# A hymba layer with a 16-expert MoE: router on unnormalized rows, shorter rank products, the first two experts preloaded

## What is computed

```python
h = h + mixed @ w_out
t = rms_norm(h, norm_ffn_g)
group_prob = softmax(t @ w_group + b_group)                 # 4 groups
gp, gi = top_k(group_prob, 1)
exp_logits = (t @ w_expert + b_expert).reshape(-1, 4, 4)    # 16 experts
ev, ei = top_k(exp_logits[chosen group gi], 2)
ew = softmax(ev) * gp
y = zeros_like(t)
for e in range(16):
    y = y + gates[:, e:e+1] * ((silu(t @ w_gate[e]) * (t @ w_up[e])) @ w_down[e])
h = rms_norm(h + y, final_norm_g)
```

## Time and profile before

| | |
|---|---|
| Time, median of 3 runs | 1294.54 us (1292.42 to 1296.68) |
| The profiled execution | 1298.6 us, with a span of 1296.7 us inside it |
| Mean granted TensorE clock | 0.931 of 2.4 GHz |
| PE busy (multiplying) | 1118.7 us, 86% of the span, 6954 instructions |
| DVE busy | 811.0 us, 63% |
| ACT busy | 619.7 us, 48% |
| POOL busy | 351.9 us, 27% |
| Moved by DMA | 208.54 MB, mean 161 GB/s |

### The profile page before, as it was taken

How to read it: one execution, slowest core, us unless ns; L and a number is a source line. 1 busy time by engine, 2 the same in 40 slices (tenths; PEclk the granted TensorE clock), 3 DMA queues, 4 the chain that set the end, 5 groups by cost and what they waited for, 6 DMA issues and landing times.

```text
span 1296.7 us, 21172 instructions
## 1 busy us (share of the span) xinstructions
PE 1118.7 (86%) x6954; PEld 887.6 (68%) x6954; DVE 811.0 (63%) x1201; ACT 619.7 (48%) x976; POOL 351.9 (27%) x230
## 2 busy tenths in 40 slices
PE   4899999999969689999999448999999999999920
PEld 4899899999957355555555337777777777777710
DVE  4697656444395454543433446788778888888828
ACT  5422111276423354433332116777667777777712
POOL 1431211122101001111112013544444445444332
PEclk9799999999979799998999659999999999999965
DMA  6365222222154500111113728785997958664056
GB/s 243 143 236 85 65 74 75 83 65 84 23 112 182 182 1 1 50 49 49 49 50 114 298 82 317 244 297 213 370 372 276 367 195 316 233 224 164 16 173 264
DMA packets 90051, 208.54 MB, mean 161 GB/s; under 512 B 8288, under 2 KB 28256, under 8 KB 89328
## 3 DMA queue, kind: packets, MB, share of 16 engines
q1 hardware_dynamic: 78464, 165.69, 37.7%
q0 software_dynamic: 8064, 29.36, 6.4%
q10 hardware_dynamic: 3456, 12.58, 2.4%
HBM read 222.71 MB, written 40.94 MB: 203 GB/s over the span
## 4 chain that ended last, share of the span: by engine, by line
PE 60%; DVE 11%; ACT 10%; issue 7%; POOL 5%; DMA 3%; SPq 2%; ACTq 1%; POOLq 0%; DVEq 0%
PE ps L462 17%; PE ps L2078 15%; PE ps L1746 9%; ACT split L2121 5%; POOL split L2040 5%; PE ps L1719 3%; PE ps L1696 3%; DVE split L2174 2%; DVE mem L2258 1%; PE ps L1713 1%; PE ps L1733 1%; PE ps L1357 1%; PE ps L537 1%; PE ps L2066 1%; ACT mem L1639 1%
## 5 line engine op out<-in xcount | busy, mean ns | idle before, releaser
L2078 PE MATMUL ps<-split 128*128 128x512 f32 x1728 | 428.0, 402 | 28.9 <-DVE split L2174 21.1
L2078 PEld LDWEIGHTS ps<-split 128*128 128x128 f32 x1728 | 321.5, 191 | 117.8 <-DVE split L2174 20.0
L2121 ACT CAST split<-weights 128x1024 fp32r x288 | 293.8, 1050 | 125.9 <-PE ps L2078 84.9
L2174 DVE TENSOR_TENSOR split<-weights,split 128x1024 fp32r<-128x1024 f32 x216 | 281.7, 1357 | 92.4 <-ACT split L2121 92.2
L462 PE MATMUL ps<-xsplit,wsplit 128*128 128x384 f32 (+2 forms) x1584 | 280.5, 333 | 6.7 <-DVE xsplit L416 6.7
L462 PEld LDWEIGHTS ps<-xsplit,wsplit 128*128 128x128 f32 x1584 | 256.9, 194 | 13.2 <-DVE xsplit L416 7.6
L2040 POOL TENSOR_TENSOR split<-weights,split 128x1024 fp32r<-128x1024 f32 x72 | 188.1, 2612 | 239.9 <-ACT split L2121 239.9
L246 POOL TENSOR_TENSOR wsplit<-mem,wsplit 128x1024 fp32r<-128x1024 f32 x22 | 57.8, 2629 | 251.3 <-ACT wsplit L315 251.3
L1746 PE MATMUL ps<-mem 128*128 128x512 f32 x256 | 119.4, 611 | 0.8 <-DVE mem L1585 0.8
L1557 DVE TENSOR_REDUCE sml<-ps 128x1 f32<-128x1040 f32 (+7 forms) x64 | 46.6, 769 | 84.9 <-PE ps L1696 84.8
L1639 ACT COPY mem<-ps 128x512 f32<-128x512 f32 (+3 forms) x48 | 21.5, 481 | 136.0 <-PE ps L1713 90.2
(11 more groups left out here) (382 smaller groups left out, 1290.2 us busy)
## 6 DMA issues: line engine op xcount, KB each, us to landing
weights<-in_w_down SPq DMA_DIRECT2D x25, 2048.0 KB, 7.8
weights<-in_w_gate SPq DMA_DIRECT2D x48, 1024.0 KB
weights<-in_w_up SPq DMA_DIRECT2D x48, 1024.0 KB
ye_d<-par ACTq DMA_DIRECT2D x24, 512.0 KB, 7.4
mem<-in_w_in SPq DMA_DIRECT2D x22, 512.0 KB, 4.1
ye_d<-mem POOLq DMA_DIRECT2D x16, 512.0 KB, 11.2
mem<-in_x SPq DMA_DIRECT2D x10, 512.0 KB, 4.3
mem<-in_w_out SPq DMA_DIRECT2D x1, 4096.0 KB, 12.9
```

The costliest lines, as they stand in the source:

```text
L2078: mm = nc.tensor.matmul(ps[:, bank + h, :], x, w[place % RING][:, 512 * h:512 * h + 512], start=(k == 0 and p_ == 0), stop=(k == n - 1 and ...
L2121: nc.scalar.copy(WH[place % RING], raw(kind, k, q)).then_inc(wh_ready, 1)
L2174: nc.vector.tensor_tensor(WL[place % RING], raw(kind, k, q), WH[place % RING].bitcast(F32), ALU.subtract).then_inc(wl_dve, 1)
```

## The change

1. The router no longer waits for the norm. PE transposes the residual rows `H1R` themselves; the norm's gain is multiplied into the router's matrix `WRT` once (POOL), and the 1/rms of each row into the logits (DVE). The last tile's "x" and "r" entries move two steps up. `XN2` is still written and stored for the experts, and SP reloads an `H1R` buffer only after its transposes were copied (`ring_free`).
2. Ranks: the counts over all tiles are summed by PE (8 products of 16 columns, bf16), and the ranks over tiles as well (8 more, of 128 down to 16 columns), in place of DVE's seven additions and copies. The one-hot tables for the row numbers are bf16, and the row number is split in two parts below 256, so that one pass is exact; the 16 products start after the first half of the table `HOTR`.
3. Experts 0 and 1 always get at least one block. Expert 1's weights are loaded into buffer 1 before the routing's tables exist, and the load tables count both as present. The first block's addresses are fixed in the program.
4. The first block's chunks are split during the routing: ACT makes the high parts of chunks 0 to 3 behind its two exponentials, DVE the low part of chunk 0 while PE counts and of chunks 1 and 2 behind the row numbers, POOL that of chunk 3. ACT no longer waits for `tables_ready` before the first block.

The core of the diff:

```diff
@@ attention
-        NSTEP = NJOB + 11
+        NSTEP = NJOB + 9
-            return ... 4 * n + {"m": 7, "x": 13, "r": 14}[kind]
+            return ... 4 * n + {"m": 7, "x": 13 - 2 * (n == NT - 1), "r": 14 - 2 * (n == NT - 1)}[kind]
 def sp_attention
                     sp.wait_ge(h1_stored[p % 2], 16 * (p // 2 + 1))
+                    sp.wait_ge(ring_free, xt_at[p])
                     sp_residual(sp, p + 2)
 def pool_attention
+            pool.wait_ge(ffn_loaded, 48)
+            nc.gpsimd.tensor_tensor(WRT, WRT, par[:, P_GMIX:P_GMIX + KD].unsqueeze(2).to_broadcast([P, KD, 20]), ALU.mult).then_inc(pool_filled, 1)
 def dve_normed
-                dve.wait_ge(ring_free, xt_at[p - 2])
 def act_square
+            if p >= 2:
+                act.wait_ge(xn2_stored[p % 2], 16 * (p // 2))
-            nc.scalar.activation(XT2[:, p % 2].rearrange("p k q -> p (k q)"), H1R[:, p % 2], ACT.Square,
+            nc.scalar.activation(XN2[:, p % 2], H1R[:, p % 2], ACT.Square,
 def pe_ring, "x"
-                pe.wait_ge(xn2_ready, n + 1)
+                pe.wait_ge(h1_ready, n + 1)
-                    mm = nc.tensor.transpose(b[:, P * j:P * j + P], XN2[:, n % 2, P * k:P * k + P], ident)
+                    mm = nc.tensor.transpose(b[:, P * j:P * j + P], H1R[:, n % 2, P * k:P * k + P], ident)
@@ def pe_route
-            nc.tensor.matmul(ps[:, 0, 0:P], con[:, C_TRI:C_TRI + P], f, start=True, stop=True)
-            nc.tensor.matmul(ps[:, 0, P:2 * P], con[:, C_ONES:C_ONES + P], f, start=True, stop=True).then_inc(rank_done, 1)
+            for t in range(NT):
+                mm = nc.tensor.matmul(ps[:, 3, 0:NE], ALL, OKB[:, t], start=(t == 0), stop=(t == NT - 1))
+            mm.then_inc(rank_done, 1)
+            nc.tensor.matmul(ps[:, 0, 0:P], BEFORE, OKB.rearrange("p t e -> p (t e)"), start=True, stop=False, skip_group_check=True)
+            for t in range(NT - 1):
+                mm = nc.tensor.matmul(ps[:, 0, NE * (t + 1):P].rearrange("p (t e) -> p t e", e=NE), ALL,
+                                      OKB[:, t].unsqueeze(1).to_broadcast([P, NT - 1 - t, NE]), start=False, stop=(t == NT - 2),
+                                      skip_group_check=True)
+            mm.then_inc(rank_done, 1)
             for n in range(2 * NT):
-                mm = nc.tensor.matmul(ps[:, 1, 0:NB], HOTR[:, n], HOTB[:, n], start=(n == 0), stop=(n == 2 * NT - 1))
+                if n == NT:
+                    pe.wait_ge(slot_hot_ready, 2)
+                mm = nc.tensor.matmul(ps[:, 1, 0:2 * NB], HOTR[:, n], HOTB[:, n].rearrange("p i b -> p (i b)"), start=(n == 0), stop=(n == 2 * NT - 1))
@@ def dve_route
-            link(tt(LG, LGR, BR.unsqueeze(1).to_broadcast([P, NT, 20]), ALU.add))
+            link(tt(LG, LGR, RS2.unsqueeze(2).to_broadcast([P, NT, 20]), ALU.mult))
+            link(tt(LG, LG, BR.unsqueeze(1).to_broadcast([P, NT, 20]), ALU.add))
+            dve_weights_lower(dve, None, 0, "gu", 0, 0)
             dve.wait_ge(rank_done, 1)
...
+            link(ts(BLK[:, 0:2], BLK[:, 0:2], 1.0, None, ALU.max))
...
-            for t in range(1, NT):
-                link(tt(PRE[:, t], PRE[:, t - 1], TOT[:, t - 1], ALU.add))
...
+            for k in range(2):
+                tt(HOTR[:, NT * k:NT * k + NT], fl[0][:, NT * k:NT * k + NT].to_broadcast([P, NT, P]),
+                   IOTAP.unsqueeze(1).to_broadcast([P, NT, P]), ALU.is_equal).then_inc(slot_hot_ready, 1)
...
+            dve.wait_ge(idx_done, 1)
+            link(ts(IXF, ps[:, 1, NB:2 * NB], float(P), None, ALU.mult))
+            tt(ixb, ps[:, 1, 0:NB], IXF, ALU.add).then_inc(slots_ready, 1)
+            for k in range(1, RING - 1):
+                dve_weights_lower(dve, None, k, "gu", k, 0)
...
-            link(ts(NEW[:, 0:1], EBF[:, 0:1], 0.0, None, ALU.is_gt))
+            link(stt(NEW, EBF, 1.5, NEW, ALU.is_gt, ALU.mult))
@@ def sp_experts
+            sp.wait_ge(out_done, NT)
+            for half in range(2):
+                for i, w in enumerate(("w_gate", "w_up")):
+                    sp.dma_start(WGU[:, KD + 4 * half:KD + 4 * half + 4, i],
+                                 a[w][1, 512 * half:512 * half + 512].rearrange("(k p) n -> p k n", p=P)).then_inc(w_loads[half], 16)
...
-            sp.wait_ge(ring_free, len(ring))
+            sp.wait_ge(ring_free, xt_at[NT - 1])
+            sp.wait_ge(first_loaded, 32)
             sp.dma_start(WDN[:, 0:FF // P], a["w_down"][0]...).then_inc(first_loaded, 16)
+            sp.wait_ge(rt_gap, 1)
+            sp.dma_start(WDN[:, FF // P:2 * FF // P], a["w_down"][1]...).then_inc(wdn_loaded, 16)
             sp.dma_start(H1, h1_d.rearrange("(t p) d -> p t d", p=P)).then_inc(late_loaded, 16)
@@ def act_experts
+            act.wait_ge(out_done, NT)
+            act.wait_ge(first_loaded, 32)
+            for k in range(RING):
+                higher(None, k, "gu", k, 0)
+            act.wait_ge(slots_ready, 1)
             copy_x(0, 0)
+            for k in range(RING, KD):
+                higher(None, k, "gu", k, 0)
+            silu(0, 0)
             act.wait_ge(tables_ready, 1)
-            act.wait_ge(first_loaded, 48)
```

More of the change, by code:

```diff
@@ L1945, in raw @@
         def raw(kind, k, q):
+            if isinstance(q, int):
+                return WGU[:, q * KD + k].rearrange("p i n -> p (i n)")
             if kind == "gu":
@@ L2001, in body @@
                 for half in range(2):
-                    if par or not first:
-                        sp.wait_ge(w_loads[half], 32 * b)
+                    sp.wait_ge(w_loads[half], 32 * b + 32)
                     sp.wait_ge(chunk_used, (free, free_second)[half])
@@ L2008, in body @@
                                      cond=new).then_inc(w_loads[half], 16)
-                if par or not first:
-                    sp.wait_ge(wdn_loaded, 16 * b)
+                sp.wait_ge(wdn_loaded, 16 * b + 16)
                 sp.wait_ge(chunk_used, free_down)
@@ L2194, in dve_experts @@
             x_lower(0, 0)
-            q0 = buffer_of(dve, 0)
-            for k in range(KD):
+            for k in range(RING, KD):
                 if k % RING < RING - 1:
-                    lower(None, k, "gu", k, q0)
+                    lower(None, k, "gu", k, 0)
             hidden(0, 0)
```

83 lines of the change are left out of this document (40 added, 43 removed).

## The result

The changed kernel takes 1280.1 us (median of 4 runs, 1276.69 to 1284.37), the kernel before, run beside it, 1295.6 us (4 runs, 1292.42 to 1298.81): the ratio is 0.9882, 95% interval 0.9838 to 0.9926. So the change gains 15 to 18 us. Single executions scatter by more than the 0.3% named at the start: the kernel before alone ran from 1282.9 to 1303.2 us beside the kernels of this document, but for one execution in a slower state (1487.97 us at a mean granted clock of 0.725), which is left out everywhere.

The account below looks back on a forecast made before the run. PE bounds the experts, so the end follows the first expert product: router 3.9 less 0.36, ranks 4.8, entry 6.6 make 14.9 us. 1298.6 becomes 1283.7; less 4.1 for the median, 1279.6 (range 1273.5 to 1286.5).

Parts of the forecast that it names:

- Router: Last tile's router on PE: not waiting for the norm gains 3.9 us, the added multiplication on the logits costs 0.36.
- Counting products: PE's 8 bf16 products of 16 columns for the ranks: 0.16 us each, 1.3 together.
- Lock: In the ranks, POOL's split of chunk 3 holds up DVE's first product of two SBUF tables: 1.8 us lost.
- The tables for the row numbers: DVE's HOT, its scaling, two halves and HOTR in two halves, ahead of the row products: 4.5 us.
- Row numbers: End of the ranks, when the row numbers are there: 747.1 us instead of 755.44, 8.3 earlier.
- Landing: First gather of rows for the experts, beside bulk loads: lands after 5.5 us, 1.0 to 1.2 more than before.
- Rival (b): The gather is late, queued among 12 MB of new bulk loads, landing 4.0 over the one assumed: 1283.4 us, chance 0.13.
- The first two experts without tables: Part of the stretch from the row numbers to the first expert product, for which 6.6 us gained was claimed.
- Rival (a): Passage lighter than reckoned: no lock cost, clock up through the router, quick small products; 4.2 less, 1275.4 us, chance 0.16.
- Rival (c): In the experts, the third expert's weights come late, costing 5 to 6 us: 1285.1 us, chance 0.05.
- (d): In the experts, weight loads set the pace after all and the gain is given back: 1294.5 us, chance 0.02.
- (e): In attention, six residual reloads behind the transposes' copies eat up the gain and 3.9 more: 1298.4 us, chance 0.02.

Follow-up runs that it names:

- after_again: The changed kernel once more, unchanged, timed against the kernel before: 1277.3 us, ratio 0.9866.
- undo_router: The changed kernel with only the router's part undone (it waits for the normalized rows again, no multiplication by 1/rms): 1283.2 us, ratio 0.9894.
- before_again: The kernel before once more, unchanged, profiled a second time: 1296.5 us (1 run).
- pool_late: The changed kernel with only POOL's split of chunk 3 moved from the routing to behind the tables: 1274.8 us, ratio 0.9840.
- splits_wait: splits_late, with ACT waiting for the tables and the first block's skipped loads before it splits, as in the kernel before: 1279.6 us, ratio 0.9905.
- best: both_late, with DVE taking the low part of the first block's rows in the middle of the tables: 1274.0 us, ratio 0.9870.
- both_late: The changed kernel with POOL's first-block splits behind gathers and tables, and the residual's 4 MB load issued behind the tables: 1274.3 us, ratio 0.9872.
- splits_late: The changed kernel with no first-block chunk split during the routing, all split after the rows are copied: 1278.7 us, ratio 0.9870.

## Why the prediction was right, and where its terms were not

The time (1280.1 and 1277.3 for 1279.6) and the passage (40.27 for 758.75 - 718.62 = 40.13) came out, with a rest 2.5 us shorter in the profiled execution. Four terms were mis-sized, three by 0.7 to 0.9 us too long and one by 2.5 too short, and cancelled: that the passage came out within 0.1 us of its sum (0.8 in after_again) is luck.

- **Router** (3.9 gained, 0.36 paid): right, 3.4 net by undo_router. Leaving the 16 products at 3.57 was the cautious bound: 2.86 and 1.93 were measured, so 0.7 and 1.6 more were gained. The sum took the fall from a row of the kernel before, at 721, 2.8 us behind the residual; in before_again the same program had it at 4.1, and in the change it came while the products ran.
- **Counting products** (8 of 0.16, 1.3 us): 0.41, and the second half of the row products (1.4) 0.61. The Trainium skill's rule (TensorE: Matmul & The Clock Gate, Back-to-back issue gap), which I had only weighed, was nearer. By it, an estimate, 0.2 us were due; measured were 0.41, 0.05 per product of 16 columns. DVE's split of chunk 0, "hides in PE's work" in my sum, then became what ends the wait: PE is done at 736.23, the split at 736.76. The nearest row, an f32 product of 32 columns, was a poor guide for bf16 products of 16. (The sum's 734.95 should also read 734.86, 732.76 + 0.80 + 1.3.)
- **Lock** (1.8 lost): 1.7, as a whole: its mechanism and its size. It hit the second product rather than the first, since DVE was there 1.6 us sooner and POOL only 0.7. The product ended 0.14 us behind POOL's split (741.12 and 740.98), and without that split, in pool_late, it took 0.29. That agrees with the Trainium skill's exclusive lock (SBUF — State Buffer, Who interferes with whom) and not with even sharing.
- **The tables for the row numbers** (4.5): 742.32 to 746.83, 4.5. The scaling with one tensor operand took 0.49 for the 0.72 taken (L1872); the rest of the sum made up for it.
- **Row numbers** (747.1, rel. 28.5): rel. 26.86, sooner by 1.6, by the terms above.
- **Landing** (5.5, "1.0 to 1.2 more"): 8.0, so 3.5 more than before. This is the step that failed. I had the bulk loads end at 755, when the gather would be nearly in; the last of them, issued at 735.81, landed 30.1 us later, at 765.9 (the queues moved some 410 GB/s until 764), so the gather stood beside them over its whole way. (Of the 12 MB that the rival called new, 6 were there before too, but had landed before that gather.) I priced it by the median of the gathers in the expert stage, where the traffic is 253 GB/s on average and not 410. Rival (b) had the mechanism. It took the landing 4.0 over the one assumed, and it was 2.5; the 1.6 won before the gather paid for most of it. POOL's copy beside DVE's split, 1.2 in my sum, was 0.8, and the product came 3.4 behind the turning of the rows instead of 3.65, since the gather and not the tables bound it. That makes 40.27 for 40.13.
- **The first two experts without tables** (inside "6.6 gained"): 4.8 measured from the row numbers to the product (18.2 before, 13.4 now). The wait for tables and skipped loads is a real price (splits_wait); the splits ahead of the routing's end are worth 0.9 at best and lose as much with POOL's.
- **Rival (a)** had two of its three parts: the clock stayed up longer (0.7 and 1.6) and the small products were quicker (0.9 and 0.8). The lock cost its full length.
- **Rival (c)**: SP issued the third expert's load at 775.31, for 773 forecast; the waits for weights rose to 7.3 us on ACT without reaching PE. **(d)** and **(e)**: the rest didn't grow, and the residual's moment is 3.24 later in the first profile, but 5.0 of delay stood there at L1226 already, ahead of the reloads, and in best, which has the same reloads, it is 3.5 sooner than in the kernel before: drift, not the reloads.

What stays open: why the residual's moment varies, by 7 us over the kernels that share the change's attention (715.13 to 722.26). Nor were all combinations tried: DVE's splits of chunks 1 and 2 (2.35 us) stand ahead of the tables, which bind in both_late, and beside POOL's index copy, which still takes 0.90 in best. Without them, in splits_late, the tables end 33.1 us behind the residual at equal clock, 35.8 in both_late; late splits together with the late residual load were not run.

## What to carry to other kernels

Where a stage waits on a chain of small operations, look at what the change puts beside the chain, not only at what it takes out of it: here one load of 4 MB and one split of 2.4 us, neither needed before the first product, cost 3.9 of the 18.0 us that the passage had to give (both_late against the kernel before, at equal clock). Issue a latency-critical small transfer ahead of bulk loads whose data is needed later, and keep GpSimd's long elementwise operations off the moments at which VectorE runs two-input operations in a chain. And when a total comes out as predicted, compare the marks on the way all the same: four terms off by 0.7 to 2.5 us gave a total off by 0.1.

## What the runs showed of the hardware that I had not expected

- A VectorE operation on 128 x 128 took 1.99 us for 0.29 beside a GpSimd split, and the other way round, a GpSimd copy of one column took 0.99 for 0.20 beside VectorE's splits: both sides can be the one that waits.
- The first gather, 128 rows of 4 KB, landed after 4.5 to 5.6 us where the bulk loads had ended before its issue or ended within 2 us behind it, after 5.8 where they ended 4 us behind it, and after 7.7 to 8.2 where they went on beyond it at some 410 GB/s.
- Eight bf16 products of 16 columns took 0.41 us and eight of 64 columns 0.61 at the granted clock of 0.50: four times the columns cost half as much again.
- The clock's fall from 2.4 to 1.2 GHz behind the last large products came at different points of the same instruction stream in different executions: the same 16 products took 1.93, 2.81, 2.86, 2.87, 2.91, 3.06, 3.50 and 3.58 us.
